# One modulation row from unsplit weights, and the query and key weights ahead of it, in a fused transformer and mixture-of-experts kernel

## The reference

```python
mod_x = jax.nn.silu(c) @ ada_w[l] + ada_b[l]
sh1, sc1, g1, sh2, sc2, g2 = jnp.split(mod_x[:, None, :], 6, axis=-1)
mod_c = jax.nn.silu(c_ctx) @ ada_w[l] + ada_b[l]          # the same weights, for the context
csh1, csc1, cg1, csh2, csc2, cg2 = jnp.split(mod_c, 6, axis=-1)
hc = modulate(rmsnorm(ctx, norm1_g[l]), csh1, csc1)       # modulate: h * (1 + scale) + shift
pc = hc @ w_in[l]
hx = modulate(rmsnorm(x, norm1_g[l]), sh1, sc1)
px = hx @ w_in[l]      # columns: 0:512 Fourier, 512:768 queries, 768:896 keys/values, 896:928 rotary keys, then gates
```

## Time and profile before

| | |
|---|---|
| median of 3 runs | 1819.91 us |
| lowest and highest run | 1819.46 and 1821.04 us |
| the profiled execution | 1819.94 us |
| its span | 1818.1 us |
| mean granted clock of TensorE | 0.967 |
| TensorE busy (PE) | 1710.0 us, 94% |
| VectorE busy (DVE) | 1193.7 us, 66% |
| ScalarE busy (ACT) | 903.6 us, 50% |

### The profile page before, as it was taken

One profiled execution on the slowest core, in us unless ns is written; L12 is line 12 of the kernel. 1 busy time (PEld: TensorE's weight loads), 2 busy tenths in 40 slices (PEclk: granted clock), 3 DMA queues, 4 the chain that ended last, 5 costly groups with the idle time before them and its releaser, 6 DMA issues.

```text
span 1818.1 us, 18644 instructions
## 1 busy us (share of the span) xinstructions
PE 1710.0 (94%) x7626; PEld 1315.8 (72%) x7626; DVE 1193.7 (66%) x1310; ACT 903.6 (50%) x995; POOL 110.9 (6%) x139
## 2 busy tenths in 40 slices
PE   5999998999999999999999998979999999999994
PEld 2767664666778888887687666868888888888882
DVE  7533546687454434343569584379999999999894
ACT  6424444443332323132533214367878878777872
POOL 0000003000000000000000230010101111010100
PEclk9999999999989999999899997979999999999998
DMA  9114451002213232322122100149999999999993
GB/s 379 47 63 178 185 183 50 1 1 93 93 48 115 93 112 85 105 93 70 51 90 92 47 1 29 70 173 368 364 372 380 378 363 362 359 372 364 386 336 150
DMA packets 54523, 322.79 MB, mean 178 GB/s; under 512 B 12577, under 2 KB 13089, under 8 KB 17826
## 3 DMA queue, kind: packets, MB, share of 16 engines
q1 hardware_dynamic: 42480, 305.81, 44.8%
q0 software_dynamic: 9216, 8.42, 1.4%
q10 hardware_dynamic: 2738, 7.33, 1.0%
HBM read 325.70 MB, written 20.97 MB: 191 GB/s over the span
## 4 chain that ended last, share of the span: by engine, by line
PE 85%; DVE 9%; ACT 3%; DMA 2%; issue 1%; POOL 0%; SPq 0%; DVEq 0%; POOLq 0%; ACTq 0%
PE ps L514 33%; PE ps L1252 18%; PE ps L1279 10%; PE ps L620 3%; DVE wlo L1897 2%; PE ps L1140 2%; PE ps L840 2%; PE ps L1238 2%; ACT whi L1340 2%; DVE scr L2177 1%; PE ps L653 1%; PE ps L906 1%; PE ps L985 1%; PE ps L943 1%; DMA xT<-in_x 1%
## 5 line engine op out<-in xcount | busy, mean ns | idle before, releaser
L1897 DVE TENSOR_TENSOR wlo<-raw,whi 128x2048 fp32r<-128x2048 f32 x284 | 642.4, 2283 | 195.8 <-ACT whi L1340 195.5
L1340 ACT ACTIVATE whi<-raw 128x2048 fp32r<-128x2048 f32 x284 | 538.1, 1913 | 197.4 <-PE ps L514 103.2
L514 PE MATMUL ps<-hH,whi 128*128 128x512 f32 x576 | 230.0, 399 | 8.4 <-DVE wlo L1897 8.4
L514 PE MATMUL ps<-hL,whi 128*128 128x512 f32 x576 | 227.2, 394 | 0.0
L514 PE MATMUL ps<-hH,wlo 128*128 128x512 f32 x576 | 227.2, 394 | 0.0
L1252 PE MATMUL ps<-whi,xH 128*128 128x512 f32 x512 | 203.5, 397 | 0.0
L1252 PE MATMUL ps<-whi,xL 128*128 128x512 f32 x512 | 201.0, 393 | 0.0
L1252 PE MATMUL ps<-wlo,xH 128*128 128x512 f32 x512 | 199.9, 390 | 0.0
L514 PEld LDWEIGHTS ps<-hH,whi 128*128 128x128 f32 x576 | 107.9, 187 | 38.3 <-DVE wlo L1897 12.2
L514 PEld LDWEIGHTS ps<-hH,wlo 128*128 128x128 f32 x576 | 107.9, 187 | 26.4
L514 PEld LDWEIGHTS ps<-hL,whi 128*128 128x128 f32 x576 | 107.9, 187 | 26.1 <-issue 0.5
(11 more groups left out here) (464 smaller groups left out, 2658.5 us busy)
## 6 DMA issues: line engine op xcount, KB each, us to landing
raw<-in_experts SPq DMA_DIRECT2D x192, 1024.0 KB, 7.4
raw<-in_streamed SPq DMA_DIRECT2D x92, 1024.0 KB, 4.8
xT<-in_x SPq DMA_DIRECT2D x1, 2048.0 KB, 17.0
h_scratch<-hN ACTq DMA_DIRECT2D x4, 512.0 KB, 2.6
Y<-y_scratch SPq DMA_DIRECT2D x4, 512.0 KB, 7.8
Y<-y_scratch ACTq DMA_DIRECT2D x4, 512.0 KB, 8.1
out<-xN SPq DMA_DIRECT2D x4, 512.0 KB, 2.6
ctxT<-in_ctx SPq DMA_DIRECT2D x1, 1024.0 KB, 18.7
```

The lines of the kernel that those rows point to most:

```text
L514: ins = e.matmul(o, l, r, start=(i == 0), stop=(i == len(prs) - 1))
L1340: e.activation(u.hi, u.raw, ACT.Copy).then_inc(*p.inc("hi", n, on="hi"))
L1897: e.tensor_tensor(u.lo, u.raw, u.hi.bitcast(F32), ALU.subtract).then_inc(*p.inc("lo", n, on="lo"))
```

## The change

Units are reordered: query and key weights become units 4 and 5, row 3's weights 6 and 7 and row 1's weights 8 and 9 (before: row 3 at 4 and 5, row 1 at 6 and 7, queries and keys at 8 and 9). Row 3's units are not split; `mod(3)` on TensorE becomes 8 float32 matmuls with 2 stationary columns (silu(c) and silu(c_ctx)) and raw weights, its row 2 x 512. The spread is issued ahead of `mod(3)`. `mod_columns(3)`, `mod(1)` and `mod_columns(1)` move into the loop over `first(k)`. ACT's and DVE's orders follow.

```diff
-    for j in MOD_FIRST:
+    for j in MOD_FIRST[0:2]:
         mod(j)
     wide("q", "w_in", 0, 8, 512, 768)
     wide("kv", "w_in", 0, 8, 768, 928)
+    for j in MOD_FIRST[2:4]:
+        mod(j)
...
+MOD_WHOLE = (3,)
...
-    half_ring = [Place(O_HL + 4096 * i) for i in range(3)]
+    half_ring = [Place(O_HL + 4096 * i) for i in (2, 0, 1)]
...
-    FIRST_RAW = {3: PH + 4096, 4: PH + 12192, 5: PH + 10144, 9: PH + 8192}
-    FIRST_HALF = {8: (PH, PH + 2048), 9: (PH + 4096, PH + 15520)}
+    FIRST_RAW = {3: PH + 4096, 4: PH + 12192, 5: PH + 8192, 6: PH + 10144}
+    FIRST_HALF = {4: (PH, PH + 2048), 5: (PH + 4096, PH + 15520)}
...
-        stream(A["streamed"][i, :, 0:w], k1 - k0, n1 - n0, name != "dfts")
+        whole = name == "dfts" or any(i in order["mod", j] for j in MOD_WHOLE)
+        stream(A["streamed"][i, :, 0:w], k1 - k0, n1 - n0, not whole)
...  (TensorE, mod)
+                if j in MOD_WHOLE:
+                    p.wait_ge(*done("dma", "u", n))
+                    p.wait_ge(*done("dve", "sil"))
+                    p.wait_ge(*done(*b.before))
+                    for k in range(4):
+                        kk = 4 * half + k
+                        ins = e.matmul(b.t[0:2, :], sil[:, kk:16:8], u.raw[:, k, :], start=(kk == 0), stop=(kk == 7))
+                    ins.then_inc(*p.inc("use", n))
+                    continue
...  (TensorE, order)
         mod_columns(0)
+        spread(0, 512, ("dve", "ns", 0, 7), hold=True)
         mod(3)
-        spread(0, 512, ("dve", "ns", 0, 7), hold=True)
-        mod(1, (0,))
-        mod_columns(3)
-        mod(1, (1,))
...
         for k in range(8):
             first(k)
             if k == 0:
+                mod_columns(3)
+            elif k == 2:
+                mod(1)
+            elif k == 3:
                 mod_columns(1)
...  (ScalarE, order)
-        convert(4)
+        convert(U_Q)
         row(0)
         root(0)
-        convert(5)
-        convert(6)
-        convert(7)
+        convert(U_KV)
+        rounded(0, range(2), T, lambda d: modc[:, d, 0:1], lambda d: hH[:, d, :])
         row(3)
-        convert(8)
-        convert(9)
-        rounded(0, range(2), T, lambda d: modc[:, d, 0:1], lambda d: hH[:, d, :])
+        rounded(0, range(2, 4), T, lambda d: modc[:, d, 0:1], lambda d: hH[:, d, :])
+        convert(U_MOD[1][0])
+        convert(U_MOD[1][1])
         row(1)
-        rounded(0, range(2, 4), T, lambda d: modc[:, d, 0:1], lambda d: hH[:, d, :])
...  (VectorE, mod: with whole weights two adds of the bias in place of copy, add and two adds)
...  (VectorE, order)
-        convert(4)
+        convert(U_Q)
         inverse(0)
         mod(0)
-        convert(5)
-        convert(6)
-        convert(7)
-        convert(8)
+        convert(U_KV)
+        norm_x(0, 4)
+        convert(U_MOD[1][0])
+        convert(U_MOD[1][1])
         mod(3)
         scale(4)
-        convert(9)
-        norm_x(0, 4)
         mod(1)
```

More of the change, by code:

```diff
@@ L374, in build @@
     table, order = unit_table()
-    third = half_ring[2]
+    third = half_ring[0]
     for i, (name, k0, k1, n0, n1) in enumerate(table):
@@ L563, in mod_columns @@
             p.wait_ge(*done(*b.before))
+            w = 2 if j in MOD_WHOLE else 4
             for i in range(4):
-                ins = e.transpose(b.t[:, 4 * i:4 * i + 4], rowbuf[:, i * 128:(i + 1) * 128], ident[0:4, 0:4])
+                ins = e.transpose(b.t[:, w * i:w * i + w], rowbuf[0:w, i * 128:(i + 1) * 128], ident[0:w, 0:w])
             ins.then_inc(*p.inc("modT", j))
@@ L1351, in row @@
                 p.wait_ge(*done("pe", "modT", MODS[MODS.index(j) - 1]))
-            e.activation(rowbuf[:, :], ps["mod", j].t[0:4, :], ACT.Copy).then_inc(*p.inc("row", j))
+            w = 2 if j in MOD_WHOLE else 4
+            e.activation(rowbuf[0:w, :], ps["mod", j].t[0:w, :], ACT.Copy).then_inc(*p.inc("row", j))
         def square(n, d, src, *before):
@@ L1907, in mod @@
             p.wait_ge(*done("pe", "modT", j))
+            b = cols("ada_b", 48)[:, 4 * j:4 * j + 4]
+            if j in MOD_WHOLE:
+                w = ps["modT", j].t[:, 0:8].rearrange("p (i c) -> p i c", i=4)
+                for q in range(2):
+                    ins = e.tensor_tensor(modc[:, 4 * j:4 * j + 4, q], w[:, :, q], b, ALU.add)
+                ins.then_inc(*p.inc("mod", j))
+                return
             if j != MODS[0]:
@@ L1913, in mod @@
             p.wait_ge(*done("dve", "mc", j, 1))
-            b = cols("ada_b", 48)[:, 4 * j:4 * j + 4]
             for q in range(2):
```

## The result

The changed kernel takes 1825.01 us (median of 13 runs, 1822.3 to 1826.86), the kernel before 1821.04 us in the 13 runs beside them (1818.25 to 1822.78): 1.0024 times, 95% interval 1.0015 to 1.0032. That is 3.97 us more. The prediction had +2.2 us on a base of 1819.94, so 1822.1, with a range to 1824.3: the direction was right, the size too small by almost half, and the measured time lies 0.7 us outside the range.

The account below looks back on a forecast made before the run. DVE's splitting was taken as the bound before 44.74 us, PE after. Earlier warm start (-2.65), row 1 (+3.7), stall (+3.2), low clock (+1.7) and transposes (+0.3) gave +2.2: 1822.1 us, range 1818.2 to 1824.3.

Parts of the forecast that it names:

- The bound and the measuring point: DVE's splitting bounds before 44.74 us, PE after; the point is the first Fourier matmul, 70.08 us, whose shift moves the end.
- Up to row 3: Start of the kernel through `mod(3)`: spread at 30.6 us, float32 records of 0.433 us, doubled at low clock, ending at 40.6.
- E: The time at which `mod(3)` ends and `first(0)` follows: 40.6 us, with 40.0 to 41.1 for other clock returns.
- From E to the Fourier columns: PE work after `mod(3)`: 15.6 us through row 1's transposes, then a 3.2 us wait and 11.2 us of matmuls.
- The new stall: Ahead of slice 4, behind row 1's later transposes: PE empty for 3.2 us until DVE's low part is finished.
- Its clock: Behind the wait ahead of slice 4: the clock falls and the low stretch loses 1.7 us.
- a surviving clock: Rival: the clock holds through the wait ahead of slice 4, ACT's copy sets the point, +1.6, 1821.5 us; chance 0.25.
- Banks and ACT: `fourier(0)` falls on the first query tile's bank and waits for ACT's copy, 71.7 us, hidden if PE arrives at 72.3.
- faster rival: Faster by over 0.2%: `mod(3)` cheap or at full clock, no clock fall at 91.0 us; -2.3 to -3.3; chance 0.07.
- The sign that later stages move by more than 2 us by themselves: Behind the Fourier columns: the prediction is wrong if later stages' waits and clock levels move by more than 2 us.
- the slower one: Rival: slower by over 0.2%, the clock returning late behind the wait ahead of slice 4; +3.7, 1823.6 us; chance 0.17.
- the saved splitting is worth nothing: Rival: DVE's saved splitting gains nothing and PE's new order costs nothing; +-0.5, 1820 us; chance 0.06.

Follow-up runs that it names:

- kernel 5: Changed kernel plus 22 and 8 unread matmuls in TensorE's two early waits; 1821.34 us, 1.0003 of the kernel before.
- Kernel 4: Kernel before with only row 3 made float32 from unsplit weights, old order of units and engines; 1823.39 us, 1.0013 of before.
- kernel 2: Changed kernel with row 3 split again, everything else as changed; 1821.71 us, 1.0005 of the kernel before.
- 10: Changed kernel with row 3 split again, mod(1) behind first(1) and its transposes behind first(2); 1820.57 us, 1.0002 of the kernel before.
- 11: Changed kernel with row 3 split, row 1 earlier, and ACT's query copies ahead of the second Fourier unit's conversion; 1819.04 us, 0.9987 of before.
- kernel 9: Kernel before with only row 1's transposes moved from behind first(0) to behind first(3); 1826.48 us, 1.0030 of before.
- 3: Changed kernel plus 12 unread matmuls in TensorE's wait ahead of slice 4 of the norm; 1823.78 us, 1.0011 of the kernel before.
- kernel 6: Changed kernel with row 1 made earlier and 22 and 8 unread matmuls in the early waits; 1817.06 us, 0.9982 of the kernel before.

## Why the prediction had the mechanism and was too small

**The bound and the measuring point** held: the point moved by 3.4 us, the last expert by 4.0, the median by 3.97.

**Up to row 3.** Spread at 30.67 (30.6), raw units there in time, 0.435 us a record at full clock (0.433). The failing step is "If the clock comes back 4.3 us after 30.6 ... it ends at 40.6". It came back 6.0 us after, at 36.7, and the first product started at 41.6: the float32 row was undersized by 1.0 us, and my outer bound of 5.3 us (E = 41.1) did not hold it. Four cases of the changed start now give 3.2, 5.5, 6.0 and 6.0 us from the resumption. The Trainium skill says in TensorE: Matmul & The Clock Gate, The HAM clock gate, that the moment at which the clock rises varies from run to run with the same kernel; the trace agrees, from 34.1 to 36.9 us here. I had built a mean and a bound from three such moments of one profile, and counted the first from a restart at 29.84 us, behind a gap of 0.81 us. Counted from the resumption behind the same 5.29 us wait, at 26.64 before and at 26.66 after, the clock came back 6.3 us later before and 10.0 us later in the changed kernel. That it stays low longer in the new order is shown, and kernel 5 shows what it costs; why it does is open. Between 29 and 32.7 us the changed kernel idles 1.62 us in place of 0.81 and runs float32 matmuls in place of split ones. Kernel 4 has the float32 row without that idle time and was low for 10.2 us as well (23.8 to 34.0); kernels 2, 10 and 11 have row 3 split, behind idle times of 1.6 and 2.1 us, and were low for 13.7 (in kernel 2 from 24.2 to 37.9). So neither of the two is the only cause.

**From E to the Fourier columns.** 15.6 us predicted to the end of the transposes, 16.0 measured (41.6 to 57.6); the tight places on ACT and DVE held without a wait. The new stall: 3.2 predicted, 3.11 measured. Its clock: 1.7 predicted, fallen at 60.6 and back at 64.0, 1.7. In all five profiles with this 3.1 us wait unfilled (changed twice, 2, 5 and 9) the clock fell, and in the one with it filled (3) it did not. Five of five speak for a chance below the 0.25 that I gave a surviving clock, though they don't rule it out. The section of the Trainium skill named there, HAM oscillation, tells it of a long wait for DMA, with the next burst starting at the low clock; that waits of 2.18 and 3.11 us for DVE can do it is shown by the rows here, and behind the 2.18 us wait the burst started at full clock and the fall came 0.9 us into it.

**Banks and ACT**: ACT's limit was predicted at 1.1 us after PE's own time without a low clock; shown as waits of 0.98 and 0.94 us in kernels 3 and 10 and removed in 11. In the changed kernel it is hidden, as written.

**The rest of the size.** Of the 1.8 us by which +3.97 exceeds +2.2, 1.0 is the float32 row, 0.2 are tenths up to the point and 0.6 came later, which no term had; in the two profiles of the changed kernel the shift grows by 0.6 and 0.4 us between the point and the last expert, and that was not traced to a cause. The remaining 1.1 us between 1822.1 and 1825.01 are the base: the three runs shown had 1819.91, thirteen have 1821.04. And my range had no term for that: on a base of 1821.04 its upper end, +4.4, would have been 1825.4, and the time inside it. At the other end, -1.7 was not the bound that my own faster rival gives, -2.3 to -3.3; and the 6.64 pieces of 1024 KB should be 6.63, on which nothing hangs. The sign that later stages move by more than 2 us by themselves was met in one of two profiles: the spans differ by 6.8 and 4.9 us, 3.4 and 1.4 more than the points.

**The rivals.** By its number the slower one, to which I gave 0.17, came true: 0.24%, with an interval from 0.15 to 0.32. It had the right kind of mechanism, a clock that comes back late, but mostly at the wrong place: it came back late in the float32 row and not behind the stall. That its +3.7 is so near the measured size is luck in part. The faster one fell. That the saved splitting is worth nothing holds for the kernel before (4); in the changed order it makes the norm earlier, but TensorE's float32 row takes more than that: the first product starts at 41.61 us, and at 39.94 with the split row (2).

## What to carry to other kernels

When work is taken from a bounding engine and given to another, write down where the other engine now stands on the path, at the clock that it has there: here 16 records cost 7.0 us at full clock and 8.9 at the mixed one, and a low clock that had cost nothing became part of the path. Before moving a small step behind other work, count what stands between it and its first reader: four transposes moved behind 36 more products opened a wait of 3.1 us and a low clock of 1.7 to 2.7 us, and moving them back ahead, with the row's own matmuls, won 4.9 us at the point. For a clock that returns at different moments take the bounds wider than the few seen, and take the base from more than three runs.

## What had not been expected

Filling two waits with matmuls that nobody reads was worth 2.7 us at the point in the changed kernel, and in time it took the loss from 4.0 to 0.7 us; in the kernel before, where no TensorE-bound stretch follows those waits, it was worth nothing in time. Even filled, the clock fell once, at 28.9 us (kernel 6), just behind 1.05 us of matmuls one column wide and the transposes. And low clock can be given back: in kernel 9 a point 6.0 us later became 4.5 us, since the next wait of 2.17 us was not followed by a fall.
